# Value products and transposes ahead of the new scores in each step of an attention pipeline (fp32, one core)

## The reference, cut to what matters

```python
def diff_attn_block(qb, keys, vals, lam):            # "diff": 4 heads, 2 maps each
    s = einsum('bqhmd,bkhmd->bhmqk', qb, keys) * DIFF_HEAD_DIM ** -0.5
    p = softmax(s)
    a = p[:, :, 0] - lam * p[:, :, 1]
    return einsum('bhqk,bkhv->bqhv', a, vals)
...
# MLA (8 heads, 96 wide) and neighbourhood attention (8 heads, 64 wide): "even"
sc = q @ k.T * scale (+ relative bias, masked)       # 256 or 512 keys
o = softmax(sc) @ v
...
# sliding window (16 heads, 2 KV heads): "swa"
parts = [sink, s_ctx, where(|q - k| <= 128, s_lat, -inf)]
p = softmax(concatenate(parts))                      # 512 keys
o = p[..., 1:] @ v
```

## Time and profile before

| | |
|---|---|
| median of 3 runs | 2779.58 us (2776.85 to 2782.95) |
| the profiled execution, its own time | 2780.0 us |
| its span, first to last instruction | 2778.2 us |
| PE busy | 2428.0 us, 87% |
| DVE busy | 697.8 us, 25% |
| ACT busy | 517.5 us, 19% |
| mean granted clock of PE | 0.943 |
| diff, even, swa (by the timeline) | 231 to 262, 1728 to 1824, 2425 to 2489 us |

### The profile page before, as it was taken

How to read it: one execution, slowest core, us unless ns; L and a number is a source line. 1 busy time by engine, 2 the same in 40 slices (tenths; PEclk the granted TensorE clock), 3 DMA queues, 4 the chain that set the end, 5 groups by cost and what they waited for, 6 DMA issues and landing times.

```text
span 2778.2 us, 37482 instructions
## 1 busy us (share of the span) xinstructions
PE 2428.0 (87%) x15842; PEld 1469.9 (53%) x15842; DVE 697.8 (25%) x1553; ACT 517.5 (19%) x1018; POOL 0.2 (0%) x4
## 2 busy tenths in 40 slices
PE   5965976999798588888888698998999999799998
PEld 1533533888687344444444343753444444678887
DVE  1137557333312311111111204621000000261001
ACT  2213032222101111111111202622000000251001
POOL 0000000000000000000000000000000000000000
PEclk8876987999899699999999899999999999899999
DMA  9510237322241488989988321011222212203431
GB/s 399 214 46 1 76 140 286 123 94 94 87 144 59 179 357 369 371 364 373 371 365 332 138 76 61 2 46 61 76 76 76 76 61 95 76 15 122 151 137 61
DMA packets 59445, 434.06 MB, mean 156 GB/s; under 512 B 6576, under 2 KB 6704, under 8 KB 7216
## 3 DMA queue, kind: packets, MB, share of 16 engines
q1 hardware_dynamic: 57744, 420.50, 38.5%
q10 hardware_dynamic: 1568, 11.58, 1.0%
HBM read 431.01 MB, written 1.05 MB: 156 GB/s over the span
## 4 chain that ended last, share of the span: by engine, by line
PE 78%; DVE 8%; DMA 8%; issue 2%; ACT 2%; SPq 0%; ACTq 0%; DVEq 0%
PE bank L513 76%; DMA ring<-in_w 7%; PE bank L620 1%; ACT normed L1160 1%; DVE arena L1531 1%; DMA sw<-in_sw 0%; DMA arena<-in_xin 0%; DVE arena L1835 0%; DVE small L1455 0%; DVE arena L1593 0%; DVE arena L1487 0%; DVE arena L1488 0%; SPq L1938 0%; DVE arena L1828 0%; DVE arena L1539 0%
## 5 line engine op out<-in xcount | busy, mean ns | idle before, releaser
L513 PE MATMUL bank<-normed,ring 128*128 128x512 f32 (+1 forms) x2688 | 879.8, 489 | 41.6 <-issue 29.5
L513 PEld LDWEIGHTS bank<-normed,ring 128*128 128x128 f32 x2688 | 518.2, 194 | 397.5 <-issue 344.9
L513 PE MATMUL bank<-arena 64*64 64x64 f32 (+6 forms) x6896 | 439.8, 251 | 50.8 <-DVEq L456 16.4
L513 PE MATMUL bank<-ring,arena 128*64 128x512 f32 (+1 forms) x1824 | 403.2, 623 | 56.6 <-DMA ring<-in_w 32.7
L513 PEld LDWEIGHTS bank<-arena 64*64 64x64 f32 (+4 forms) x6896 | 361.2, 146 | 137.0 <-issue 105.1
L513 PE MATMUL bank<-arena,ring 128*128 128x256 f32 (+1 forms) x1024 | 298.5, 453 | 2.8 <-DVE arena L1891 1.3
L513 PEld LDWEIGHTS bank<-ring,arena 128*64 128x64 f32 (+1 forms) x1824 | 138.8, 136 | 295.4 <-issue 241.2
L513 PEld LDWEIGHTS bank<-arena,ring 128*128 128x128 f32 x1024 | 194.2, 190 | 105.5 <-issue 84.4
L513 PE MATMUL bank<-arena,con 128*128 128x256 f32 (+5 forms) x304 | 101.7, 472 | 57.8 <-DVE arena L1532 33.6
L1891 DVE TENSOR_TENSOR arena<-arena,bank 128x512 f32<-128x512 f32 (+1 forms) x44 | 24.4, 554 | 431.6 <-PE bank L513 431.6
L513 PE MATMUL bank<-ring,normed 128*32 128x512 f32 (+2 forms) x576 | 115.0, 589 | 7.1 <-DMA ring<-in_w 7.0
(11 more groups left out here) (280 smaller groups left out, 1349.0 us busy)
## 6 DMA issues: line engine op xcount, KB each, us to landing
ring<-in_w SPq DMA_DIRECT2D x401, 1024.0 KB, 7.3
arena<-in_xin ACTq DMA_DIRECT2D x1, 2048.0 KB, 11.4
arena<-in_nab ACTq DMA_DIRECT2D x1, 2048.0 KB, 11.8
con<-in_con ACTq DMA_DIRECT2D x1, 1600.5 KB, 6.9
sw<-in_sw ACTq DMA_DIRECT2D x1, 1280.0 KB, 10.4
sw<-in_sw ACTq DMA_DIRECT2D x1, 1168.0 KB, 13.7
arena<-in_xin ACTq DMA_DIRECT2D x1, 1024.0 KB, 12.9
out<-arena ACTq DMA_DIRECT2D x1, 1024.0 KB, 4.0
```

What stands on the lines that cost most here:

```text
L513: return nc.tensor.matmul(o, l, r, start=start, stop=stop, **kw)
```

## The change

On PE the block of the scores moves from the head of the step to its end, so that a step is transposes of u-2, values of u-3, scores of u. On ACT the copies of u-2 move ahead of the exponentials of u, which keeps the order of ACT's reads equal to the order of PE's jobs. DVE's program is the same. The diff, whole but for repeated lines:

```diff
@@ PE, attention
                 for u in range(n + 3):
-                    if u < n:
-                        it = pairs[u]
-                        for sem, count in it["need"]:
-                            pe.wait_ge(S(sem), count)
-                        js = [job("act"), job("act")]
...
-                        for x in range(2):
-                            done(js[x], last[x])
-                        scored[name].append(([reads["act"][-2], reads["act"][-1]], gave["act"]))
                     if 0 <= u - 2 < n:
                         it = pairs[u - 2]
                         for x in range(len(it["pv"])):
...
                         done(j, last)
+                    if u < n:
+                        it = pairs[u]
+                        for sem, count in it["need"]:
+                            pe.wait_ge(S(sem), count)
+                        js = [job("act"), job("act")]
...
+                        for x in range(2):
+                            done(js[x], last[x])
+                        scored[name].append(([reads["act"][-2], reads["act"][-1]], gave["act"]))
@@ ACT, attention
                 for u in range(n + 2):
+                    if 0 <= u - 2 < n:
+                        it = pairs[u - 2]
+                        for x in range(len(it["pv"])):
+                            b = a.take()
+                            a.given(f(it["t"][x][:, 0:it["nk"]], b[:, 0:it["nk"]], ACT.Copy))
                     if u < n:
                         it = pairs[u]
                         for x in range(2):
...
-                    if 0 <= u - 2 < n:
-                        it = pairs[u - 2]
-                        for x in range(len(it["pv"])):
-                            b = a.take()
-                            a.given(f(it["t"][x][:, 0:it["nk"]], b[:, 0:it["nk"]], ACT.Copy))
```

More of the change, by code:

```diff
@@ L595, in attention @@
                 for u in range(n + 3):
-                    if u < n:
-                        it = pairs[u]
-                        for sem, count in it["need"]:
-                            pe.wait_ge(S(sem), count)
-                        js = [job("act"), job("act")]
-                        last = [None, None]
-                        for c in range(0, it["nk"], SEQ):
-                            for x in range(2):
[L604 to L611, removed]
-                            done(js[x], last[x])
-                        scored[name].append(([reads["act"][-2], reads["act"][-1]], gave["act"]))
                     if 0 <= u - 2 < n:
@@ L634, in attention @@
                         done(j, last)
+                    if u < n:
[3 more added lines that the diff above has]
+                        js = [job("act"), job("act")]
+                        last = [None, None]
+                        for c in range(0, it["nk"], SEQ):
+                            for x in range(2):
+                                l, r = it["qk"][x]
+                                biased = it["bias"] is not None and c == CTX
+                                last[x] = mm(banks[js[x][0]][:, c:c + SEQ], l, r[:, c:c + SEQ], True, not biased)
+                        if it["bias"] is not None:
+                            for x in range(2):
+                                o, far = it["bias"][x]
+                                last[x] = mm(banks[js[x][0]][:, o:o + far.shape[1]], ident, far, False, True)
+                        for x in range(2):
+                            done(js[x], last[x])
+                        scored[name].append(([reads["act"][-2], reads["act"][-1]], gave["act"]))
             def out_proj(src, n, name):
```

## The result

The changed kernel takes 2900.59 us (median of 4 runs, 2898.94 to 2903.34) for 2781.26 of the kernel before on the same chip: a ratio of 1.0431, 95% interval 1.0413 to 1.0449. It is slower by 119 us. The forecast was 2906 us in a range of 2866 to 2945. The profiled execution took 2901.95 us, 122 more than the 2780.0 of before.

A forecast was written before the change was run, and what follows sets the result against it. TensorE was taken to bound even and swa, VectorE diff. Bare gaps 35 + 42 + 16 = +93 us, with +33 for the clock, gave +126 on 2780.0: 2906 us, range 2866 to 2945.

The forecast's parts named there:

- The mechanism: Attention stages: transposes of u-2 directly follow scores u-1, so scores, maxima, scaling, transposes become a loop in every step.
- The signs named: Changed profile: some 95 us idle before transposes at L1477 and L1473, swa period at least 6.2 us, PE busy about 84%.
- Swa, +35 of bare gap: Stage swa: 15 gaps of 2.58 us, 38.7 us, less waits already there; net +35 us at an undisturbed clock.
- Diff, +16: Stage diff: gap 3.0 us, period 5.6 for 2.97, so 2.65 us more for some 6 steps, +16 us.
- Even, +42: Stage even: 31 gaps of mean 1.42 us, between 1.14 and 1.71, less 1.83 us present idle; +42 us.
- The clock, +33: PE's clock falling in gaps, four steps of five at 1.4 us: swa +21, diff +8, even +4; together +33 us.
- Two falls in even: Stage even: gaps of 1.1 to 1.7 us let PE's clock fall only twice, +4 us.
- ScalarE's new order costs nothing: ACT's copies of u-2 ahead of exponentials of u: covered by values and scores; without that cover 1.08 us per step.
- nothing outside the stages moves: Outside attention: no stage changes by more than a few us, otherwise the forecast counts as wrong.
- Rival 1: Attention stages: the clock holds in gaps of at most 3 us; +93, 2873 us; chance 0.27.
- Rival 2: Diff and swa: the clock stays low throughout, at half speed; +173, 2953 us; chance 0.12.
- Rivals 3 and 4: Attention gaps: 3, gaps close and it is faster, 2769 us, chance 0.02; 4, gaps half hidden, +50, 2830 us, chance 0.03.

The follow-up runs named there:

- experiment 2: Changed kernel with value products of u-3 put ahead of the transposes of u-2 on TensorE, ScalarE's order as changed: 2844.68 us, ratio 1.0241.
- 5: Changed kernel with VectorE scaling the tiles of u-1 before it takes the maxima of u: 2811.07 us, ratio 1.0118.
- 6: Kernel before, TensorE and ScalarE order untouched, with VectorE scaling u-1 before the maxima of u: 2810.34 us, ratio 1.0118.
- experiment 7: One extra unused maximum over 256 columns per pair on VectorE: kernel before 2785.9 us, ratio 1.0029; changed kernel 2953.87 us, ratio 1.0634.
- experiment 8: Changed kernel with the extra maximum, gaps filled with 13 (diff), 11 (swa), 6 or 4 (even) identity products: 2904.08 us, ratio 1.044.
- experiment 4: Changed kernel with TensorE's gaps filled by 11 (diff), 9 (swa), 5 or 3 (even) unread identity products: 2878.69 us, ratio 1.0359.
- experiment 10: Kernel before with unread identity products where TensorE idles: ahead of diff, in the fills of diff and swa, behind n6, ahead of swa: 2770.03 us, ratio 0.9957.

## Why the prediction was right, point by point

- **The mechanism** (the transposes stand behind maxima that need the scores just made) is shown from four sides: PE waits for L1477 and L1473; one block of some 1.0 us put between takes 1.02 off the gap (experiment 2); with VectorE's order turned, PE's order is without effect on the total (5 and 6); an extra maximum on VectorE costs 7 us in one order and, with the clock held, 25 in the other (7 and 8), of which the three stages have 6.8 and 15.8.
- **The signs named**: idle time before the transposes 101.3 us, where it was 9.3 (forecast some 95), period 6.24 (at least 6.2), PE busy 85% (about 84), VectorE's idle time before the maxima, released by PE. PE's idle time in a step of swa is 2.41 and not 2.6, and PE's busy time is 0.2 us longer in its place.
- **Swa, +35 of bare gap**: the period at full clock is 6.24 us, forecast 6.18. With the fitted fill the stage is 36.4 us longer than before (100.65 for 64.26).
- **Diff, +16**: the gap is 2.95 us, forecast 3.0. With the fill the stage is 13.8 us longer (45.22 for 31.42), though the fill also warms the clock from the start, which the kernel before hadn't.
- **Even, +42**: this was too small. The stage grew by 51.1, and by 50.9 with the gaps filled, so it isn't the clock of the steady steps. A round of four steps takes 17.82 us in the MLA half, 6.0 more than before, and 18.02 in the neighbourhood half, 6.4 more, where my four gaps made 5.7. The mean of the shortest and the longest gap was the wrong price for the neighbourhood steps of 256: the maxima start at 1844.32, when the scores have ended (1844.29), where in MLA they start at 1790.75, 0.40 us before the end of the scores (1791.15), and PE idles 1.30 and 1.44 us where MLA has 0.98 and 1.11. That is 4 x 0.7 + 4 x 0.3, some 4 of the missing 9 us. Another 2.9 are in the first round: from the first score to the fifth group of transposes it takes 24.05 us (1750.25 to 1774.30) where it took 15.14 (1728.11 to 1743.25), 8.9 more. The first transposes can't start before the first scaling, and scores 2 now come behind them, for which I made no term; some of these products also ran at the lower clock.

```profile
1788.99 1.09 PE L513 MATMUL bank<-arena,sw 128*64 128x128 f32 x16
1790.02 1.13 PE L513 MATMUL bank<-arena 96*128 96x256 f32 x4
1790.75 0.86 DVE L1455 TENSOR_REDUCE small<-bank 128x1 f32<-128x256 f32 x2 [2.24 <-PE bank L513]
...
1792.12 0.70 PE L602 MATMUL bank<-con,arena 128*128 128x128 f32 x4 [0.98 <-DVE arena L1477]
...
1842.56 1.73 PE L513 MATMUL bank<-arena 128*64 128x128 f32 x20
1844.32 0.75 DVE L1455 TENSOR_REDUCE small<-bank 128x1 f32<-128x256 f32 x2 [2.24 <-PE bank L513]
...
1845.59 0.70 PE L602 MATMUL bank<-con,arena 128*128 128x128 f32 x4 [1.30 <-DVE arena L1477]
```

- **The clock, +33** was too large: 20 to 22. It was 1.4 us a step in swa by forecast and is 0.8: the 14 periods from 2506.82 to 2605.17 have a mean of 7.03 for 6.24. I took a fall in four gaps of five, and half of the groups of transposes ran at the lower level. In diff the mean period is 7.0 (five periods from 245.83 to 280.86) for a computed 5.6, as forecast; the fill takes 9.5 us off the stage for a forecast of 8. (The forecast's "mean of 0.84 over a second" is one over a microsecond.) Two falls in even was near (clock 0.98), but experiment 7 shows on what edge that stood.
- The two errors, 9 us too little in even and 10 to 13 too much for the clock, offset each other; 2906 for 2901 is in part luck.
- **ScalarE's new order costs nothing**: that was right (experiment 2, where the period is PE's work and the wait for VectorE). So was that nothing outside the stages moves.
- Rival 1 (the clock holds, 2873 us) has a kernel now, experiment 4 with 2879 us. It falls for the change itself. Rival 2 (the clock stays low through diff and swa, 2953 us) falls too: half of the groups of transposes in swa ran at full clock. Rivals 3 and 4 fall with the gaps: none closed, and none was half hidden.

## What to carry to other kernels

In a software pipeline over several engines, an order is right when each product has other work between it and the next thing the engine needs from its reader; count that cover in microseconds (3.6 here) against the reader's chain (2.6), including what stands ahead of it in the reader's own program. An order that looks oldest-first on one engine is a serial loop if another engine is newest-first, so look at all the orders before one is changed. Here the mixed order of before was the fastest of the four: PE's order alone turned costs 119 us, VectorE's alone or both together 31 to 34, because scaling first closes another loop through ScalarE. A gap on TensorE has two prices, the idle time and the clock; the second is found by filling the gap with products that nobody reads, sized by their own measured length, and placed where the idle time begins.

## What the runs showed of the hardware that I had not expected

- The clock falls in shorter gaps than I thought: with gaps of 1.0 to 1.5 us (even in the changed kernel) it stays at 0.98 of full; with the same steps and gaps of 1.2 to 1.9 us it is 0.74, and the same 800 instructions take 136.23 us for 103.02. A gap of 1.39 us in each period of 5.21 (swa in experiment 2) brought no fall after the first step. The section "HAM oscillation — how this bites in real kernels" of the Trainium skill's page "TensorE: Matmul & The Clock Gate" describes it for waits of 3 to 5 us; here gaps of 2.41 us brought it down in half the steps of swa.
- A product of the identity with itself, 128 by 128 in fp32, took 0.23 us and stands as two in the trace; a transpose of the same shape through the same array took 0.13.
- Products that nobody reads made a kernel 50 us faster (experiment 8 against 7) and the kernel before 10.5 us faster (experiment 10).
